# Mixture-of-experts stage of a decoder layer: gathered rows made one pair of experts ahead, scatters spread over gate/up

## The reference

```
combine[t, e] = weight of expert e for token t      # 2 of 16 experts per token, in one group of 4
h[e]  = silu(x @ w_gate[e]) * (x @ w_up[e])         # 2048 -> 512, for each expert
h[e]  = h[e] * combine[:, e]
out   = sum over e of h[e] @ w_down[e]              # 512 -> 2048
x     = layer_norm(ALPHA * x + out) * ln2_g + ln2_b
```

## Time and profile before

| | |
|---|---|
| median of three runs | 1324.62 us |
| profiled execution | 1324.77 us |
| its span, first to last instruction | 1323.0 us |
| TensorE busy | 99% of the span |
| mean granted TensorE clock | 0.998 of full |
| VectorE, ScalarE, GpSimd busy | 43%, 36%, 2% |
| HBM read | 361.97 MB |

### The profile page before, as it was taken

One profiled execution on the slowest core, in us unless ns is written; L12 is line 12 of the kernel. 1 busy time (PEld: TensorE's weight loads), 2 busy tenths in 40 slices (PEclk: granted clock), 3 DMA queues, 4 the chain that ended last, 5 costly groups with the idle time before them and its releaser, 6 DMA issues.

```text
span 1323.0 us, 17817 instructions
## 1 busy us (share of the span) xinstructions
PE 1308.1 (99%) x7375; PEld 961.4 (73%) x7375; DVE 569.5 (43%) x737; ACT 478.5 (36%) x672; POOL 27.6 (2%) x55
## 2 busy tenths in 40 slices
PE   9999999999999999999999999999999999999898
PEld 8999989998888888888888888844453444534443
DVE  4367445456555645464555555525112121211206
ACT  4434344346556544454333433432121121211212
POOL 1000000400000000000100000000000000000000
PEclk9999999999999999999999999999999999999999
DMA  9965555544444446554556795799999999999995
GB/s 306 344 226 186 181 191 190 191 160 160 159 159 159 159 146 197 182 174 159 188 193 190 289 391 188 265 413 397 421 421 428 427 427 428 427 428 427 427 414 217
DMA packets 113987, 364.97 MB, mean 276 GB/s; under 512 B 12227, under 2 KB 19843, under 8 KB 97030
## 3 DMA queue, kind: packets, MB, share of 16 engines
q1 hardware_dynamic: 107318, 359.08, 72.8%
q10 hardware_dynamic: 6608, 5.02, 1.3%
HBM read 361.97 MB, written 2.10 MB: 275 GB/s over the span
## 4 chain that ended last, share of the span: by engine, by line
PE 89%; DMA 7%; DVE 2%; ACT 1%; issue 0%; ACTq 0%; DVEq 0%
PE main L1311 19%; PE main L1313 19%; PE main L1312 19%; PE main L605 7%; DMA mtwo<-in_expert_w_down_dram 7%; PE att L729 6%; PE main L620 6%; PE att L548 4%; PE att L1552 1%; PE main L560 1%; PE att L698 1%; PE main L561 1%; DVE wlo L1954 1%; PE att L1535 1%; PE att L1571 1%; PE att L1567 1%
## 5 line engine op out<-in xcount | busy, mean ns | idle before, releaser
L1954 DVE TENSOR_TENSOR wlo<-raw,whi 128x2048 fp32r<-128x2048 f32 x135 | 310.6, 2301 | 360.1 <-ACT whi L1712 360.1
L1712 ACT ACTIVATE whi<-raw 128x2048 fp32r<-128x2048 f32 x135 | 258.0, 1911 | 420.6 <-PE main L1313 418.6
L1311 PE MATMUL main<-whi,xhi 128*128 128x512 f32 (+1 forms) x544 | 203.8, 375 | 0.0
L1313 PE MATMUL main<-whi,xlo 128*128 128x512 f32 (+1 forms) x544 | 201.7, 371 | 0.0
L1312 PE MATMUL main<-wlo,xhi 128*128 128x512 f32 (+1 forms) x544 | 201.5, 370 | 0.0
L1311 PE MATMUL main<-xhi,whi 128*128 128x256 f32 (+1 forms) x560 | 159.6, 285 | 1.1 <-DVE wlo L2085 0.7
L1313 PE MATMUL main<-xhi,wlo 128*128 128x256 f32 (+1 forms) x560 | 158.4, 283 | 0.0
L1312 PE MATMUL main<-xlo,whi 128*128 128x256 f32 (+1 forms) x560 | 158.4, 283 | 0.0
L605 PE MATMUL main<-mtwo,xg 128*64 128x512 f32 x640 | 139.8, 594 | 0.4 <-DMA mtwo<-in_expert_w_up_dram 0.3
L1313 PEld LDWEIGHTS main<-whi,xlo 128*128 128x128 f32 x544 | 102.5, 188 | 17.7
L1311 PEld LDWEIGHTS main<-whi,xhi 128*128 128x128 f32 x544 | 102.5, 188 | 17.2
(11 more groups left out here) (337 smaller groups left out, 1406.4 us busy)
## 6 DMA issues: line engine op xcount, KB each, us to landing
raw<-in_w_in_dram SPq DMA_DIRECT2D x95, 1024.0 KB, 5.1
mtwo<-in_expert_w_gate_dram SPq DMA_DIRECT2D x20, 2048.0 KB, 26.9
mtwo<-in_expert_w_up_dram SPq DMA_DIRECT2D x20, 2048.0 KB, 28.7
mtwo<-in_expert_w_down_dram SPq DMA_DIRECT2D x18, 2048.0 KB, 28.1
raw<-in_w_branch_dram SPq DMA_DIRECT2D x24, 1024.0 KB, 5.1
mtwo<-in_expert_w_gate_dram SPq DMA_DIRECT2D x24, 1024.0 KB, 10.7
mtwo<-in_expert_w_up_dram SPq DMA_DIRECT2D x24, 1024.0 KB, 10.0
mtwo<-in_expert_w_down_dram SPq DMA_DIRECT2D x24, 1024.0 KB, 12.8
```

Of the source, the lines that this page charges most:

```text
L1311: pe.matmul(o, ah, bh, start=start, stop=False, skip_group_check=skip)
L1313: return pe.matmul(o, al, bh, start=False, stop=stop, skip_group_check=skip)
L1712: act.activation(whi[:, u % SPLIT, 0:n], raw[:, slot, 0:n], ACT.Copy).then_inc(hi_done, 1)
L1954: dve.tensor_tensor(wlo[:, u % SPLIT, 0:n], raw[:, slot, 0:n], whi[:, u % SPLIT, 0:n].bitcast(F32), ALU.subtract).then_inc(lo_done, 1)
```

## The change

Four edits, all in the order of work on TensorE and ACT; loads, buffers and DVE's order are as they were.

1. Gathers. The first pair's four gathers stand where they stood. From then on the gathers of pair m+1 are made in pair m: 0 and 1 after gate/up and its last scatter, before the transposes of h; 2 and 3 after the transposes, before down. Gathers 2 and 3 write the banks that block 3's scatters use and wait for the adds of them (sc_free).
2. Down. Before the first product into att[c], f = 0, TensorE waits for ACT to have copied the next pair's gather c out of it (xg_out), in place of one wait for sc_free.
3. Scatters. put(c) follows quarter c of gate/up, and the slot weights follow put(2).
4. ACT. The copies of the gathers move with them: 0 and 1 before the hT copies, 2 and 3 after them.

The last pair's down and its 4 KB rows stay as they are.

```diff
+                def products(h, w):
...
...
-                pe.wait_ge(hot_ok, 1 + m)
-                put(0)
-                gather(0)
-                put(1)
-                gather(1)
-                put(2)
-                if small_units:
-                    gate_up_fine(0)
+                def quarter(i):
+                    if small_units:
+                        gate_up_fine(i)
+                    else:
+                        products(i // 2, i % 2)
...
+                last = turns is not None and turns[0] == "last"
+                if fixed == 0:
+                    pe.wait_ge(hot_ok, 1)
+                    gather(0)
+                    gather(1)
+                    quarter(0)
+                    gather(2)
+                    quarter(1)
+                    gather(3)
+                    weights()
+                    quarter(2)
+                    quarter(3)
                 else:
-                    gate_up(0)
-                gather(2)
-                if small_units:
-                    gate_up_fine(1)
-                if fixed != 0:
-                    pe.wait_ge(y_lo, m * 4)
-                gather(3)
...
-                if small_units:
-                    gate_up_fine(2)
-                    gate_up_fine(3)
-                else:
-                    gate_up(1)
-                put(3)
+                    for c in range(4):
+                        quarter(c)
+                        put(c)
+                        if c == 2:
+                            weights()
+                if not last:
+                    pe.wait_ge(hot_ok, 2 + m)
+                    gather(0)
+                    gather(1)
                 for j in range(2):
                     pe.wait_ge(h_ok, 1 + j + m * 2)
...
                     ins.then_inc(ht_ps, 1)
+                if not last:
+                    for q in (2, 3):
+                        if fixed != 0:
+                            pe.wait_ge(sc_free, m * 8 + q - 2)
+                        gather(q)
...
                     for c in range(4):
-                        if f == 0 and c == 2:
-                            pe.wait_ge(sc_free, 1 + m * 8)
+                        if f == 0:
+                            pe.wait_ge(xg_out, 5 + c + m * 4)
...
+            def gathered(m, q):
+                act.wait_ge(xg_ps, 1 + q + m * 4)
+                for k in range(4 * q, 4 * q + 4):
+                    ins = act.activation(xg[:, k, :], att[:, q, k % 4 * P:(k % 4 + 1) * P], ACT.Identity,
+                                         bias=gbX[:, KT + k:KT + k + 1], scale=gbX[:, k:k + 1])
+                ins.then_inc(xg_out, 1)
...
                 act.activation(wsl[:], main[1][:, 1, 0:S], ACT.Copy)
+                if not final:
+                    gathered(m + 1, 0)
+                    gathered(m + 1, 1)
                 for j in range(2):
                     act.wait_ge(ht_ps, 1 + j + m * 2)
...
+                if not final:
+                    gathered(m + 1, 2)
+                    gathered(m + 1, 3)
                 for c in range(3 if final else 4):
```

More of the change, by code:

```diff
@@ L590, in arrived @@
                         pe.wait_ge(landed_, value)
[L592 to L601, removed]
-                            for a in range(2):
[L603 to L608, removed]
+                def products(h, w):
+                    for kk in range(8):
+                        k = 8 * h + kk
+                        if kk % 4 == 0:
+                            if w == 0:
+                                pe.wait_ge(xg_out, 1 + k // 4 + m * 4)
+                            for a in range(2):
+                                arrived(4 * h + 2 * w + a, kk // 4)
+                        for a in range(2):
+                            src = tile(4 * h + 2 * w + a, kk // 4)
+                            half = slice(a * SLOTS, (a + 1) * SLOTS)
+                            ins = pe.matmul(main[0][half, w, :], xg[:, k, half], src[:, kk % 4 * DE:(kk % 4 + 1) * DE],
+                                            start=(k == 0), stop=(k == KT - 1))
+                            if kk == 7:
+                                ins.then_inc(m_used, 1)
                 def gate_up_fine(q):
@@ L656, in step, with weights @@
-                if small_units:
-                    gate_up_fine(2)
-                    gate_up_fine(3)
-                else:
-                    gate_up(1)
-                put(3)
+                def quarter(i):
[3 more added lines that the diff above has]
+                        products(i // 2, i % 2)
+                def weights():
+                    pe.wait_ge(cmb_ok, 1 + m)
+                    pe.wait_ge(sc_free, 1 if fixed == 0 else m * 8 - 1)
+                    for t in range(T):
+                        pe.transpose(main[1][:, 1, t * P:(t + 1) * P], hot[:, t, :], ident[:])
+                    for t in range(T):
+                        ins = pe.matmul(main[1][:, 1, S:S + 2], cmb[:, t, :], ones[:, 0:2], start=(t == 0), stop=(t == 1),
+                                        skip_group_check=True)
+                    ins.then_inc(ws_t, 1)
@@ L664, in step @@
                     cols = hh[:, j * 256:(j + 1) * 256]
-                    if small_units or (turns is not None and turns[0] == "last"):
+                    if small_units or last:
                         cols = cols.rearrange("p (i f) -> p i f", i=2)
@@ L671, in step @@
                     ins.then_inc(ht_ps, 1)
-                if turns is not None and turns[0] == "last":
+                if not last:
[3 more added lines that the diff above has]
+                        gather(q)
+                if last:
                     pe.wait_ge(l1_in, 80)
@@ L769, in exponents @@
                 act.activation(ed[:], ed[:], ACT.Exp).then_inc(ed_out, 1)
-            def pair_step(m, final, first=False):
[L772 to L781, removed]
+            def gathered(m, q):
[4 more added lines that the diff above has]
+                ins.then_inc(xg_out, 1)
+            gathered(0, 0)
+            exponents()
+            gathered(0, 1)
+            act.activation(warm[:, 2:3], rowok[:], ACT.Silu)
+            gathered(0, 2)
+            gathered(0, 3)
+            def pair_step(m, final, first=False):
                 act.wait_ge(ws_t, 1 + m)
```

## The result

| | kernel before | changed kernel |
|---|---|---|
| median of 18 runs | 1323.90 us | 1326.28 us |
| lowest to highest | 1322.46 to 1325.16 | 1325.66 to 1327.78 |
| ratio, 95% interval | | 1.0019 (1.0012 to 1.0025) |
| span of the profiled execution | 1323.0 | 1323.9 |

The changed kernel is 2.4 us slower (1326.28 - 1323.90), which the interval puts at 1.6 to 3.3. So stretches are compared inside a trace. The changed kernel's gate/up of the second half starts at 881.24, before at 882.18; TensorE's times and the issues of after read 0.9 early against the prediction's. From that start to the start of the last down it is 1289.94 - 882.18 = 407.76 before and 1290.88 - 881.24 = 409.64 after: 1.9 more.

The account below looks back on a forecast made before the run. It took the weight stream, not TensorE, as the bound: +2.3 us for the late unit 17, 0 for the spread scatters, 0 for the last down's 4 KB pieces; 1324.62 + 2.3 = 1326.9 us, range 1323.4 to 1329.4.

Parts of the forecast that it names:

- What bounds: Whole kernel: the weight stream sets the end; a pair needs 58.9 us of transfers, 54.66 us of TensorE.
- Part 1, the shift of the first down: First pair: gathers placed around the transposes make down start 6.0 us later, at about 904.1, TensorE losing nothing.
- Its price: Weight queue near 907: unit 8's buffer is released late, unit 17 issues at 907.8 into a dry queue; +2.3 us.
- The Trainium skill's figure: Landing time of unit 17's first half: 4.4 us instead of the traced 5.0 would make the shift 1.5.
- Dry again?: Weight stream from the second down on: it does not run dry again, as each later pair adds queued work.
- Part 2: Scatters after each gate/up quarter: TensorE takes 0.8 us more a pair, hidden by the stream; cost 0, 1.0 in hand.
- A: Rival: TensorE is the bound, so the hT wait's removal saves 4.0 us, adds take back 1: 1321.6; chance 0.08.
- B: Rival: the stream later closes small holes worth 3.4 us and pays back the bubble: 1324.6; chance 0.17.
- C: Rival: late TensorE work or clock dips in the last pair, 1.5 to 3.0 us on top: 1329.2; chance 0.15.

Follow-up runs that it names:

- after_pe6: Changed kernel with six float32 128x128 identity products added on TensorE after put(1) in pairs two to eight: 1330.80 us, ratio 1.0051.
- experiments 2, 3 and 6: In that order the runs pair0_old, before_late17 and after_pe2: 1323.40, 1327.28 and 1326.02 us.
- after_again: Changed kernel timed and profiled once more, no edit: 1325.97 us, ratio 1.0016 against the kernel before.
- after_pe2: Changed kernel with two float32 128x128 identity products added on TensorE after put(1) in pairs two to eight: 1326.02 us, ratio 1.0017.
- before_late17: Kernel before, with only unit 17's issue held until the first pair's third fourth of down (f=2) is done: 1327.28 us, ratio 1.0027.
- late17_f1: Kernel before, with only unit 17's issue held until the first pair's second fourth of down (f=1) is done: 1325.08 us, ratio 1.0009.
- pair0_old: Changed kernel, but first pair makes no gathers for the second, which runs in old order up to its transposes: 1323.40 us, ratio 0.9999.
- before_l1g: Kernel before, with SyncE's wait for unit 18 ending at the first of L1007's two instructions, so it issues earlier: 1323.12 us, ratio 0.9997.

## Why the prediction was right

- **What bounds.** Right: the stream's last first-half down unit set the end in both kernels and in every experiment but after_pe6. No step went by the chain's 89% for TensorE.
- **Part 1, the shift of the first down.** 6.0 forecast, 5.7 measured (21.66 - 15.96). The new waits on xg_out cost 0, as forecast. The next gate/up starts at 916.68 + 0.94 = 917.6, forecast 918.0.
- **Its price.** Unit 17 at 907.5 on the clock of before (forecast 907.8), landing after 5.0 (my +2.3 lay near the 2.1 that 5.0 gives). +2.3 forecast, +2.4 and +2.1 measured. That these agree so closely is in part luck. My terms were 3.6 at unit 17 (912.8 for 909.2) less the 1.2 of unit 18. In the trace unit 17 lost 2.2, because unit 16's last half had landed only 0.4 after unit 17's issue and not 1.0 before it; unit 18's 1.2 came back as forecast; and 0.7 at unit 19, which I took to follow without a gap, made up for part of the difference. In the other three profiles of this order the first term is 1.9 to 3.1 and the last 0.8 to 0.9. The stretch 900 to 920 carried 338 GB/s, 42 less than before (forecast some 50). One detail was wrong without weight: I had unit 18 wait for f=1 as a whole, but only its second half does, and the first went at 908.70 on acc_ok alone. Both halves of unit 17 were in the queue by then.
- **The Trainium skill's figure** ("DMA: Bandwidth & Descriptors", Anatomy of one DMA), an estimate of 4.4 for a transfer of this size by the fit for GpSimd's transfers, is below all that these runs show from SyncE's queue: 5.0, 5.0, 5.1, 5.4.
- **Dry again?** No: 421 and 428 in the later windows, as in before.
- **Part 2.** +0.8 a pair forecast, +1.0 measured (55.66), mostly the wait for the adds, 1.00 for 0.9, and the scatters, of which one with the return to gate/up takes 1.13 (931.79 to 932.92) for 1.04. Its cost was 0, with 1.18 in hand at the last down for the forecast 1.0. But the path there wasn't the forecast one. I let the last quarter start when its up unit lands; in the trace it landed at 1280.60, and the quarter started at 1280.75 because the gate quarter (from 1270.92, behind the gate unit), its scatter, the wait for the adds of 0.91 and the slot weights ended then. The landing I started from, 1279.7, also held the single hole of 1.0 of that profile.
- **A** (TensorE is the bound) fell with experiments 2, 3 and 6. **B** (paid back) fell: the rates stay at 421 in 922 to 1000 and 409 in 1270 to 1290 in both kernels, although the changed one has more queued (unit 21, issued at 920.3, took 12.1 to land there, and 8.2 in before). Against 428 this is 78 x 7/428 = 1.3 us in the one stretch, 0.9 in the other. Most of it isn't holes but the pace of the transfers: halves of 1024 KB landed 2.48 to 2.49 apart (422 GB/s), whole units 4.89 to 4.90 (428), the 2 MB transfers of the last down in rows of 4 KB 5.12 (410), in both traces.
- **C** (slower by TensorE at the end, or by the clock) didn't occur: the granted clock in 1240 to 1270 and in 1270 to 1290 is 1.00 in the changed kernel, and in after_pe6, whose end TensorE sets, too. The waits of 1.67, 1.58 and 1.18, with 8 and 19 us between them, brought no dip. The case that the Trainium skill tells of ("TensorE: Matmul & The Clock Gate", HAM oscillation), where a DMA wait makes the next burst start cold, has longer waits than any here; my reading, that by it all four waits of the last pair would cost 1.5 each, took it too far. Waits of 2.6 to 2.8 do bring a dip in these traces, but not each time (last section).
- **The absolute time**, 1326.9 against 1326.28, is off by the base: the three runs of before had 1324.62 as median, eighteen have 1323.90.

## What to carry to other kernels

When TensorE is 99% busy and the transfers are at their rate too, compare the time that each needs for one period; the faster one has slack that its busy share doesn't show. Then a reordering is judged by when it releases buffers, at the moment when the queue of loads is shortest, and not by the work that it saves or adds. Exchanging work that takes the same time can cost what the queue then runs dry, and the mend may be as small as leaving one iteration in its old order. Here that brought the kernel back to the time of before, and not below it by more than the noise.

## What the runs showed of the hardware that wasn't expected

- A load of 1024 KB issued when the queue had at most 0.9 us left to land (unit 17 in after, after_again, after_pe2, after_pe6 and before_late17) landed after 5.0, 5.1, 5.0, 5.3 and 5.1 us; with 1.5 us left after 5.4 (late17_f1). Unit 18 took 5.9 with 2.3 us left (before), 7.1 with 3.5 left (late17_f1), both 1.1 to 1.2 later than the pace, but 5.1 with 2.5 left and on the pace in pair0_old. So a queue with a few us left is no surety that the next load follows without a gap. While the queue stays filled, halves follow each other at 2.48 to 2.49.
- A wait of TensorE for down weights was followed by a dip of the clock, 32 matmuls in 8.62, 8.79 and 8.53 us, after an idle of 2.80 (before), 2.59 (before_l1g) and 2.70 (late17_f1). It was not, 32 matmuls in 7.09, after 2.80 (late17_f1 again), 2.80 and 2.86 (before_late17). After idle times up to 1.97 (before_l1g, 1239.76) none was seen. So the length of such a wait doesn't tell by itself whether the clock falls; what does was not found. From late17_f1's timeline, whose mean granted clock in 1183 to 1186 was 0.70:

```profile
1181.86 8.53 PE L731 MATMUL att<-mtwo,hT 128*64 128x512 f32 x32 [2.70 <-DMA mtwo<-in_expert_w_down_dram]
...
1241.20 7.09 PE L731 MATMUL att<-mtwo,hT 128*64 128x512 f32 x32 [2.80 <-DMA mtwo<-in_expert_w_down_dram]
```

- What a single late load costs the stream at 907 shows at 1290 at its size: 5.7 us of lateness, 1.7 to 2.0 us lost there, 1.9 at the last down and 2.1 to 2.4 in the run's time; 6.9 us of lateness, 3.2 lost, 3.4 in the time. No run showed any of it given back.
